# Halo tiles in pairs, weights cast by the load, norm gains applied at the transposes: an eight-core macaron decoder layer

## The reference

```
h = x + 0.5 * rms(swiglu(rms(x, g1), w1_in, w1_out), g1post)     # first FFN, hidden width 2816
u = rms(h, gmix)
q, k, v of mixers A and B, q of M  =  split(u @ w_in)             # rope on q and k of A and B
o_a = three dilated windows (128,1) (512,4) (2048,16), merged by their softmax sums
o_b = window of 128 keys with sinks;   o_m = attention to 256 memory tokens
merged = sum over a, b, m of  sigmoid(u @ w_gate + b) * (o @ w_o)
h = h + rms(merged @ w_out, gmixpost)
y = h + 0.5 * rms(swiglu(rms(h, g2), w2_in, w2_out), g2post)      # second FFN
```

## Time and profile before

| what | value |
|---|---|
| median of 3 runs | 3979.47 us (3976.4 to 3980.2) |
| the profiled execution, its own time | 3981.11 us |
| its span, core 2 | 3979.5 us |
| busy PE / DVE / ACT / POOL | 90% / 45% / 27% / 23% |
| DMA moved | 707 MB, 178 GB/s on average |

### The profile page before, as it was taken

One profiled execution on the slowest core, in us unless ns is written; L12 is line 12 of the kernel. 1 busy time (PEld: TensorE's weight loads), 2 busy tenths in 40 slices (PEclk: granted clock), 3 DMA queues, 4 the chain that ended last, 5 costly groups with the idle time before them and its releaser, 6 DMA issues.

```text
span 3979.5 us, 55960 instructions; the slowest of 8 cores (3769.7 to 3979.5 us)
## 1 busy us (share of the span) xinstructions
PE 3600.1 (90%) x19182; PEld 1792.1 (45%) x19182; DVE 1796.3 (45%) x2870; ACT 1084.1 (27%) x1885; POOL 896.4 (23%) x1135
## 2 busy tenths in 40 slices
PE   4679998988868989998999899989998999899878
PEld 1334444444323444454445444544454445544544
DVE  3433444366454553356335633563356335633543
ACT  2322232223332233223322332233223312331231
POOL 3420112141442302040204020402040203120320
PEclk9889999999989999999999999999999999999889
DMA  7974666454888634463456345634463446344544
GB/s 214 319 264 151 191 204 206 151 188 157 282 286 283 230 105 150 154 217 102 149 158 212 105 150 158 213 105 151 158 212 106 148 154 211 122 151 145 189 125 133
DMA packets 182253, 707.05 MB, mean 178 GB/s; under 512 B 20560, under 2 KB 20816, under 8 KB 168784
## 3 DMA queue, kind: packets, MB, share of 16 engines
q1 hardware_dynamic: 159936, 623.87, 48.9%
q0 software_dynamic: 22032, 79.50, 6.3%
HBM read 631.80 MB, written 71.83 MB: 177 GB/s over the span
## 4 chain that ended last, share of the span: by engine, by line
PE 76%; DMA 12%; DVE 5%; issue 3%; POOL 2%; ACT 2%; SPq 0%; DVEq 0%; POOLq 0%; ACTq 0%
PE ps L353 75%; DMA wslot<-wf 8%; DMA wslot<-wsc 2%; PE ps L541 1%; ACT mix L363 1%; POOL wslot L383 1%; DMA xs<-xh 1%; DVE mix L374 1%; DVE ps L378 1%; DVE h L374 1%; DVE mix L663 1%; DVE mix L874 1%; POOL rstd L374 1%; PE ps L899 0%; DVE wslot L383 0%
## 5 line engine op out<-in xcount | busy, mean ns | idle before, releaser
L353 PE MATMUL ps<-xn,wslot 128*128 128x512 bf16 (+1 forms) x10128 | 2273.0, 380 | 96.4 <-DVE wslot L383 39.6
L353 PEld LDWEIGHTS ps<-xn,wslot 128*128 128x128 bf16 x10128 | 1000.6, 99 | 1237.0 <-issue 205.9
L378 DVE SCALAR_TENSOR_TENSOR tsig<-tsig,ps 128x512 f32<-128x512 f32 (+1 forms) x440 | 296.0, 673 | 644.1 <-ACT tsig L363 643.6
L353 PE MATMUL ps<-wslot,hid 128*128 128x512 bf16 x2068 | 463.1, 384 | 44.0 <-DVE wslot L371 22.5
L363 ACT ACTIVATE tsig<-ps 128x512 f32<-128x512 f32 (+1 forms) x440 | 256.3, 583 | 805.0 <-PE ps L353 804.8
L378 DVE SCALAR_TENSOR_TENSOR ps<-ps,rstd,gpost_sb 128x1024 f32<-128x1024 f32 x109 | 140.8, 1291 | 612.3 <-POOL rstd L374 612.3
L363 ACT ACTIVATE mix<-ps 128x512 bf16<-128x512 f32 (+3 forms) x350 | 227.2, 680 | 660.2 <-PE ps L353 648.0
L383 POOL TENSOR_SCALAR rstd<-ssq 128x1 f32<-128x1 f32 x236 | 52.1, 221 | 1567.0 <-ACT q L363 1020.8
L353 PEld LDWEIGHTS ps<-wslot,hid 128*128 128x128 bf16 x2068 | 201.7, 99 | 302.1 <-issue 71.0
L353 PE MATMUL ps<-wslot,mix 128*128 128x512 bf16 x1364 | 298.7, 381 | 7.2 <-DVE wslot L371 4.9
L374 POOL TENSOR_TENSOR q<-mix 128x512 bf16<-128x512 f32 (+1 forms) x144 | 218.4, 1516 | 201.6 <-DVE mix L663 126.2
(11 more groups left out here) (95 smaller groups left out, 2529.6 us busy)
## 6 DMA issues: line engine op xcount, KB each, us to landing
wslot<-wsc SPq DMA_DIRECT2D x779, 512.0 KB, 4.2
wslot<-wf SPq DMA_DIRECT2D x80, 1024.0 KB, 9.3
wsc<-wslot SPq DMA_DIRECT2D x95, 512.0 KB, 9.3
wslot<-wsc SPq DMA_DIRECT2D x56, 576.0 KB, 3.8
xs<-xh POOLq DMA_DIRECT2D x47, 512.0 KB, 5.0
h<-xh POOLq DMA_DIRECT2D x47, 512.0 KB, 14.0
y<-h POOLq DMA_DIRECT2D x31, 512.0 KB, 7.9
mix<-wf SPq DMA_DIRECT2D x15, 1024.0 KB, 13.1
```

The source lines that it names most:

```text
L353: P.add("pe", lambda e: e.matmul(outV.ap, lhsT=lhsV.ap, rhs=rhsV.ap, start=start, stop=stop, skip_group_check=True), reads=[lhsV, rhsV], w ...
L378: P.add("dve", lambda e: e.scalar_tensor_tensor(out=outV.ap, in0=aV.ap, scalar=sc, in1=bV.ap, op0=op0, op1=op1), reads=[aV, bV] + ([scalar ...
```

## The change

Staging and the cast instructions go. A piece that is not yet in `wsc` is loaded by POOL's DMA queue straight from f32 DRAM into its bf16 slot, the DMA converting. FFN pieces are stored to `wsc` when their first use is released; the others are loaded by cast at their first two uses and stored when the second is released. The norm gains, formerly multiplied into the weights, are multiplied at the DVE copy behind the transposes. 17 of the 22 `f2_i` pieces are cast DRAM to DRAM during the halo phase (`w_ahead`). Tiles 0 and 1, then 2 and 3, take each first-FFN `i` piece together (`f_in_pair`, 32 matmuls for a piece); in `two` the second matrix of one tile fills the boundary of the other. The memory part moves behind tile 0's projection. Four slots more come at `w_open`, behind the last halo projection. At the start SP loads the x blocks of two tiles, and POOL's first weight loads wait for them (`gates`); role 0 has 11 slots from the start. The diff's core ("..." marks what is left out):

```diff
+def stored_at(role, nm):
+    return 0 if nm[0] == "f" else 1
...
-        stage_w = [sub(wring, (7 + 2 * k) * PE_ * 2, PE_ * 4, F32) for k in range(2)]
-        stage_m = sub(mix, 0, PE_ * 4, F32)
-        W = dict(free=list(range(7)), stage=[stage_w[0], stage_w[1], stage_m], next=0, use=0, cast=set(), at={}, staged=[], store=[],
-                 halo=True, opened=False)
...
+        xn3 = sub(wring, 7 * PE_ * 2, 8192, BF16)
+        xtH = sub(wring, 7 * PE_ * 2 + 8192, 8192, BF16)
+        W = dict(free=list(range(7 if NHALO else NSLOT)), next=0, use=0, at={}, done={}, stored=set(), ahead=0, gates=[])
+        uses = {n: seq.count(n) for n in PT} if seq else {}
...
+                n = W["done"].get(nm, 0)
+                if nm not in W["stored"] and n > stored_at(role, nm):
+                    return
+                s = W["free"].pop(0)
+                W["done"][nm] = n + 1
+                if nm in W["stored"]:
                     dma("sp", slots[s].ap[:, 0:used], wsc[PID[nm]][:, 0:used], ("wslot", s), reads=[dk("wsc", nm)],
                         writes=[slots[s].v(0, used)])
-                    W["at"][W["next"]] = s
+                else:
+                    gate = [W["gates"].pop(0)] if W["gates"] else []
+                    dma("pool", slots[s].ap[:, 0:used], wf[PID[nm]][:, 0:used], ("wcast", s), reads=gate, writes=[slots[s].v(0, used)])
+                W["at"][W["next"]] = (s, n)
...
+        def w_ahead(nm):
+            if dry:
+                return
+            used = piece_cols(nm)
+            k = W["ahead"] % 4
+            W["ahead"] += 1
+            assert nm not in W["done"]
+            W["stored"].add(nm)
+            dma("pool", wsc[PID[nm]][:, 0:used], wf[PID[nm]][:, 0:used], ("ahead", k), writes=[dk("wsc", nm), dk("ahead", k)])
...
-            W["free"].append(W["at"].pop(k))
-            w_store()
-            if len(W["staged"]) > 1 or (W["staged"] and not W["stage"]):
-                w_cast()
-            w_pump()
-        dma("sp", gpre.ap, gpred.rearrange("p a b -> p (a b)"), "c_gpre", writes=[gpre.v(0, 32)])
-        dma("sp", bgate.ap, bgated, "c_bg", writes=[bgate.v(0, 24)])
-        dma("sp", esink.ap, sinksd.partition_broadcast(128), "c_sink", writes=[esink.v(0, 4)])
-        act(esink.v(0, 4), esink.v(0, 4), AF.Exp)
-        P.add("dve", lambda e: e.memset(nhalf.ap, -0.5), writes=[nhalf.v(0, 1)])
-        P.add("dve", lambda e: e.memset(ones.ap, 1.0), writes=[ones.v(0, 128)])
-        ts("dve", bgate.v(0, 24), bgate.v(0, 24), 0.5, ALU.mult)
+            s, n = W["at"].pop(k)
+            nm = seq[k]
+            used = piece_cols(nm)
+            if nm not in W["stored"] and n == stored_at(role, nm) and n + 1 < uses[nm]:
+                W["stored"].add(nm)
+                dma("sp", wsc[PID[nm]][:, 0:used], slots[s].ap[:, 0:used], ("st", s), reads=[slots[s].v(0, used)], writes=[dk("wsc", nm)])
+            W["free"].append(s)
+        def w_open():
+            if not dry:
+                W["free"] += range(7, NSLOT)
...
+            if eng == "act":
+                act(o_, x_, AF.Copy, scale=rs)
+            else:
+                ts(eng, o_, x_, rs, ALU.mult)
...
-            cp("dve", dst, View(p16.rearrange("p (c t) -> p c t", t=128), [("ps", b)]))
+            g_ = View(gpre.ap[:, gain * 8:(gain + 1) * 8].unsqueeze(2).broadcast_to([128, 8, 128]), gpre.v(gain * 8, (gain + 1) * 8).keys)
+            tt("dve", dst, View(p16.rearrange("p (c t) -> p c t", t=128), [("ps", b)]), g_, ALU.mult)
...
+        def f_in_pair(jobs, pool):
+            for f in range(NF):
+                k, wt = use("f1_i%d" % f)
+                got = []
+                for c0 in (0, 128):
+                    for (xn, hid) in jobs:
+                        b = bank(pool)
+                        for c in range(8):
+                            mm(pv(b), wt.v(c * 256 + c0, c * 256 + c0 + 128), xn.v(c * TT, (c + 1) * TT), c == 0, c == 7)
+                        got.append(b)
+                        if c0 == 0:
+                            j = nxt("t", 3)
+                            t = tb_.v(j * TT, (j + 1) * TT)
+                            act(t, pv(b), AF.Tanh, scale=0.5)
+                            stt(t, t, 1.0, pv(b), ALU.add, ALU.mult)
+                            got[-1] = t
+                        else:
+                            tt("dve", hid.v(f * TT, (f + 1) * TT), got[len(got) - 3], pv(b), ALU.mult)
+                        if len(got) == 4:
+                            release(k)
+                        yield
...
+        if NHALO:
+            x0 = [xs.v(0, D), xs.v(D, 2 * D), cst.v(0, D), tb_.v(0, D)]
+            for r in range(4):
+                dma("sp", x0[r].ap, x_rows(0, r), ("x0", r), writes=[x0[r]])
+            for r in range(4):
+                load_h(1, r, "sp")
+            W["gates"] = [x0[1], x0[3], hT.v(3 * D, 4 * D)]
...
+            prep = prep_iter(2)
+            for _ in f_in_pair([(xn1, hid1), (xn2, hid2)], (0, 1, 2, 3, 4, 5, 6, 7)):
+                step(prep)
+            drain(prep)
+            late = ["f2_i%d" % f for f in range(NF)]
+            def two(a, b, a_groups, a_with_b, a_middle, b_middle, prep):
+                load_cst(a)
+                edge = Boundary(*F1, 4, G_MIX, xtH)
+                f_out(1, hid2, 4, edge, a_middle)
+                out_b = None
+                nxt_edge = Boundary(*F1, 4, G_MIX, xtH)
+                out_b = f_out_units(1, hid1, 4, nxt_edge)
+                def more():
+                    step(out_b)
+                    for _ in range(4):
+                        step(prep)
+                edge.tail(more)
+                for r in range(4):
+                    load_x(b, r)
+                more()
+                pj[0] = ODD
+                project(a, False, a_groups, a_with_b)
+                load_cst(b)
+                b_middle()
+                pj[0] = PJ
+                drain(out_b)
+                return nxt_edge
...
+            prep = prep_iter(3)
+            edge = two(1, 0, (2,), False, lambda: t_pre(2, xn1, ODD), lambda: t_pre(3, xn3, ODD), prep)
+            F[0] = f_in_pair([(xn1, hid1), (xn3, hid2)], FIN4)
+            edge.tail(lambda: fill(4))
+            for r in range(4):
+                load_x(3, r)
+            project(0, False, (2,), False)
+            memory_prep()
+            fill(6)
+            memory()
+            prep = prep_iter(4)
+            n = 0
+            while F[0] is not None:
+                fill(1)
+                step(prep)
+                n += 1
+                if n % 4 == 0 and late:
+                    w_ahead(late.pop(0))
+            drain(prep)
+            edge = two(3, 2, (0, 1, 2), True, lambda: t_pre(4, xn1, ODD), lambda: None, iter(()))
+            F[0] = f_in_units(1, xn1, hid1, TILES[4][0])
+            edge.tail()
+            for r in range(4):
+                load_x(4, r)
+            project(2, False, (2,), False)
+            w_open()
```

More of the change, by code:

```diff
@@ L226, with piece_cols @@
 PID = {n: k for k, n in enumerate(PNAMES)}
[L228 to L236, removed]
+def piece_cols(nm):
+    return sum(n * sum(c[1] for c in cols) for (_, _, n, cols, _) in PT[nm][1])
+def stored_at(role, nm):
+    return 0 if nm[0] == "f" else 1
 def build_program():
@@ L404, in w_cast @@
[L404 to L418, removed]
-                for j, (lo, n, k) in enumerate(merged_rows):
-                    eng = ("dve", "act", "dve", "pool")[j % 4]
-                    o_, i_ = slots[s].v(lo, lo + n), sg.v(lo, lo + n)
-                    if k is None:
-                        cp("dve", o_, i_)
-                    elif eng == "act":
-                        act(o_, i_, AF.Copy, scale=gpre.v(g * 8 + k, g * 8 + k + 1))
-                    else:
-                        ts(eng, o_, i_, gpre.v(g * 8 + k, g * 8 + k + 1), ALU.mult)
-            W["at"][W["staged_idx"].pop(0)] = s
-            W["store"].append((nm, s, used))
-            if sg is not stage_m or W["halo"]:
-                W["stage"].append(sg)
@@ L466, in use @@
             w_pump()
-            while k not in W["at"]:
-                assert W["staged"], (nm, W["free"])
-                w_cast()
-                w_pump()
-            return k, slots[W["at"][k]]
+            assert k in W["at"], (nm, W["free"])
+            return k, slots[W["at"][k][0]]
         def release(k):
@@ L633, in tail @@
                 self.turn(z)
-                fill(1)
+                more()
         def load_x(i, r):
@@ L1093, in trace @@
-            edge.tail()
-            if own:
-                load_gpost(1)
-            if not own:
-                if not last:
-                    for r in range(4):
-                        load_x(i + 1, r)
-                project(i, False, (0, 1, 2) if i == NHALO - 1 else (2,), i == NHALO - 1)
-                prep = prep_iter(i + 2) if i + 2 < NTILE else iter(())
+            load_cst(i)
+            if NHALO and i == NHALO:
+                prep = prep_iter(i + 1)
```

(9 more changed lines are left out.)

188 lines of the change are left out of this document (93 added, 95 removed).

## The result

The changed kernel takes 3879.88 us, the median of four runs (3859.75 to 3908.1), where the kernel before took 3979.84. The ratio is 0.9733 (95% interval 0.9671 to 0.9796): faster, and inside the range, but by the ratio only some 106 us were gained of the 165 forecast. In some executions the four cores of one die show a lower granted clock and take some per cent longer; ratios leave these out, and the other die's cores are read. The profiled execution took 3863.72 us.

A forecast was written before the change was run, and what follows sets the result against it. PE bounds the steady tiles, bringing in weights the cold ones. 3979.5 - 75 (halo stretch) - 106 (first own tile) + 5 (second own tile) + 10 (gains at transposes) = 3813.5, forecast 3814 us, range 3755 to 3885.

The forecast's parts named there:

- the smaller-gain rival: First two own tiles: POOL's store waits reach PE through the rope additions, costing 60 us, 3874 us in all; chance 0.23.
- the sum of the halo stretch: Start to tile 4's projection: 40 start, 629 matmuls, 23 transposes, 66 stalls give 758 us, where it was 833.
- Queues: Weight loads moved from SP to POOL: POOL lags PE by one store, 9.3 us, inside the own tiles' 10 and 5.
- a pair stretch with PE below 95%: Paired first-FFN tiles: listed as a sign of error; forecast was 234 matmuls per 50 us until 190.
- POOL's lag reaches PE: Rope of the first two own tiles: 5 us at twelve places, 60 us, 3874 in all; chance 0.23.
- The start: Kernel start: x blocks in at 21.5 us, first full matmul work at 40 instead of 49.4, between 34 and 50.
- the stall between tile 1's halves: Tile 1's second matrix: slots must be stored before reloading, 7 MB in 22 us, a stall of 17 (13 to 25).
- at 161 GB/s the first pair's 143 us: Pair of tiles 0 and 1: even casting at half the plain rate, its 150 us of matmuls would cover the loads.
- The slow rival: POOL's casting loads run one after another, 9.3 us per MB, losing 200 us: 4014 us; chance 0.06.
- the gained copy at the high end: DVE copy behind the transposes: 1.225 us against 0.684, plus 0.54 each, 10 us in all (0 to 18).
- it does nothing by itself: Pairing of tiles: no gain alone, since tiles 1 to 3 already ran within 7 us of PE.
- the second sign of being wrong: Rope additions on POOL released by a store, listed as evidence against the forecast.

The follow-up runs named there:

- Run 3: Changed kernel with norm preparation stepping at every second pair unit and x loads of tile 3 and memory rows issued earlier; 3821.13 us, ratio 0.9591.
- run 4: Changed kernel with x loads of the norms of tiles 2, 3, 4 and memory rows issued by SP instead of POOL; 3825.47 us, ratio 0.9582.
- run 8: On Run 3: two weight loads, POOL's roots, then five loads; fewer gates; key/value pieces stored at first use; memory loads further ahead; ratio 0.9583.
- run 10: Changed kernel with the norm gains left out, a plain copy behind the transposes; ratio 0.9727.
- run 9: On Run 3, tiles 0 and 1 go through the first matrix one after the other; no ratio, profiled execution 3840.4 us.

## Why the prediction was right, and where it failed

The result lies in the range because the range reaches past the smaller-gain rival; of the forecast's own terms, three of four came out, and the total missed by 66 us. That it is inside is in part luck.

**The step that failed is the sum of the halo stretch**, 758. Its two wrong terms:

*A term that was missing: the preparation of the next norms.* "Queues" says what is queued behind POOL's weight loads, "the roots of the boundaries and the rope and merge additions", and that PE meets the lag "in the rope additions only". The x loads of the prepared norms are on the same queue, and were left out, and so was what waits for them: ACT, with the tanh behind. In the first pair it is the root of the block before that stands ahead of each x load on POOL, more than the weight load between (an issue of 0.61 us); at tile 1's boundary the weight load of the projection stands behind roots and x loads. The halving of a unit, which halves the lead of each load, was in the diff and was not costed. Run 3 takes this cause away and reaches 761; run 4 does so by the queue alone. So it is worth 47 to 49 us on the four cores, nearly all of the 52 that were lacking. One of the prediction's own signs of being wrong shows it, a pair stretch with PE below 95%: 43.50 of 50 us from 60 to 110. The rival "POOL's lag reaches PE" had the size nearly (3874), at the wrong place: at the rope, in the own tiles, which came out as forecast.

*The start: 40 forecast, 51.7 measured* (core 6), just beyond its bound of 50. The x blocks were in at 32.1, not at 21.5: SP's last issue of them stands at 12.51, and its load took 19.58 us. In run 8 an earlier start was paid for later.

Run 3 keeps its start at 52 and still ends at 761, so the other terms of the stretch together were some 9 us too dear. One of them: the stall between tile 1's halves, 17 in the sum (13 to 25), is 13.4 in run 3 on core 3, and its working (stores before reloads) is about a third of it.

One bound was reckoned wrong, without effect: at 161 GB/s the first pair's 143 us are the reads alone; with the 11.5 MB of stores at 322 GB/s it would be 179, over the 150 of its matmuls.

**Right:** the casting load at the plain rate per byte read (8.6 us for the MB). The slow rival's loads, one after another, are not seen: of five that POOL issued from 232.95 us on (four of 1 MB read, one of half), the last landed at 256.4, so 5.2 us for each MB, not 9.3. Right too: the gained copy at the high end, 1.217 us against 1.23. By the Trainium skill's rule (VectorE: DVE Perf Modes, the perf-mode tier table) a two-tensor operation with a PSUM operand runs at one element per cycle where a copy may run at two, and the row agrees, 1.217 us against the copy's 0.684. First own tile 409.1 against 410; second own tile 2.9 dearer against 5; the rest 9.6 against 10, which is closer than single executions can tell (run 10). Pairing pays where pieces are cast: 33 us in run 9. That it does nothing by itself stays argued; the pair of tiles 2 and 3, whose pieces are cast no more, was not undone.

**Partly open:** the chain holds at tile 4's projection. Core 6 shows

```profile
823.95 16.25 DMA wsc<-wslot
841.79 7.18 DMA wsc<-wslot
```

two stores that POOL's casting loads wait for, behind which its rope additions stand. This is the mechanism of the rival "POOL's lag reaches PE", and the second sign of being wrong, at one place of the twelve; run 3 has it as well (17.12 and 8.97 on core 3). Run 8 takes it away together with other things, and puts it at 6 to 10 us; no run takes it away alone.

## What to carry to other kernels

When loads move to another engine's queue, list everything that this engine issues, small loads too, and follow each to the engine that will stand at it; an x load that kept ACT waiting 5.7 us, for a norm that was not needed until a tile later, cost PE 2.9 us through ACT's order. When a loop's unit changes size, look for what counts in units: a lead of two steps was 7 us and became 3.4. And compare the same cores before and after: the slowest core before and after was another, and made the halo's gain look like 28 us where it was 12 in the profiled executions.

## What the runs showed of the hardware

An idle DMA system and a starving PE stand side by side: 0.48 busy and 150 GB/s in a stretch where PE works 32 of 50 us. A plain x load from SP landed in 7.8 us where POOL's took 6.7 in the same window, and the kernel was 1.5% faster with it. A cast from DRAM to DRAM takes longer than one into a slot, 23.7 us in the median for 17 pieces on core 6, beside 8.6. No matmul waited for one, but POOL did: ten waits for an earlier one to land before the next was issued, 60.5 us together, all behind the last x load of that loop.
